# Features as 128k+p instead of 8p+k, and the work around it, in a two-layer diffusion backbone

## The chip, the cores and the metric

One Trainium2 chip, one core, one launch. The metric is the device time of the program in microseconds.

## What is computed

128 context tokens and 128 latent tokens of width 1024 go through two layers: HGRN2 (a gated linear recurrence, both directions), then neighbourhood attention, each followed by a mixture of experts; all in fp32. Cut to what the change touches:

```python
for l in range(2):
    sh1, sc1, g1, sh2, sc2, g2 = split(silu(c) @ ada_w[l] + ada_b[l], 6)     # one set for each token group
    x = x + g1 * mixer_l(rmsnorm(x, norm1_w[l]) * (1 + sc1) + sh1)
    h = rmsnorm(x, norm2_w[l]) * (1 + sc2) + sh2
    scores = sigmoid(h @ w_router)            # 64 experts, 8 groups, top 4 groups, top 6 experts
    hid = silu(h @ w_gate[e]) * (h @ w_up[e]) # 1024 -> 256 for each expert
    x = x + g2 * (sum_e((hid * combine[e]) @ w_down[e]) + shared_swiglu(h))
y = rmsnorm(x, final_norm_w)
```

## The kernel before

The activations stand transposed, features on partitions: `xT` and `hT` are [128, 8, 256], chunk k of partition p holds feature 8p+k, and the 256 columns are the two token groups. So weights are loaded as `(p k) n`, and where a product makes new features its stationary operand takes every eighth column: `late[:, h, k::K]` in `project_out`, `ws_dn[:, c, k::K]` in `shared_down`, `y[:, j, part, k::K]` in `combine`. An fp32 matmul is two records in the trace.

HGRN stage: blocks of `hgrn_w_in` and halves of the modulation weights `ada_w` (2 MB each) pass through a ring of five rooms. The table `ROUNDS` says which block, which items of the recurrence and how many modulation halves PE does in each round. `ada` is PE's part, `modulation` DVE's.

MoE (`experts_front`, `experts_pass`): `experts_front` turns `hT` into token rows, splits them into three bf16 parts (`h_tok`), routes and does the shared expert. Then 32 pairs of experts, 48 token slots each in half of the array, double buffered in `ring`. A pair on PE, in `down` and `gate_up`: gather of the next pair's tokens (48 bf16 matmuls of 96 columns), turn of `hid` (2 transposes of `hid[:, j, c::2]`), combine of the pair before (24 bf16 matmuls of 256 columns into PSUM banks 0 to 3), `turn_hots` (the one-hots times an identity, and times the 6 weight columns), down (8 fp32 matmuls of 512 columns), gate_up (32 of 256 columns). ACT does the silu and the high and middle parts of `y`, DVE the product `hid`, the rests of `y` and the next one-hots. SP loads gate and up of pair n+2 when `gate_up(n)` is done, and down when its product is done. After the last pair PE waits for the last part of `y` and does a combine, DVE adds the residual, ACT squares.

The end of the program: squares, `norm_sums` over all features broadcast to 128 partitions, root, reciprocal, products, gains, 16 transposes, four strided copies into `y_tok`, two DMAs from ACT's queue. Matmuls issued by the helper `mm` are L1288 in every view, ACT's copies L543; L1617 is the turn of `hid`, L885 the residual, L1170 `hid`, L840 the reciprocal, L554 the root, L393 SP's gate and up loads.

## Time and profile before

| | us |
|---|---|
| median of three runs | 1531.21 |
| lowest, highest | 1530.73, 1533.91 |
| profiled execution | 1534.29 |
| its span | 1532.5 |
| PE busy in it | 1485.4 |
| its mean granted clock of TensorE | 0.989 |

The profile comes from one execution, whose time stands 3.1 us above the median. Busy time overlaps where engines work beside each other. The two MoE stages take from about 273 to 815 us and from 972 to 1515 us of the span.

### The profile page before, as it was taken

To read this page: it belongs to the slowest core of one execution; us is meant where nothing else is said; L and a number is where in the kernel's file an instruction comes from. 1 tells how busy PE (TensorE), PEld (TensorE's weight loads), DVE (VectorE), ACT (ScalarE), POOL (GpSimd) and SP (SyncE) were. 2 spreads that over 40 slices of the span, in tenths; PEclk is the share of its full clock that TensorE was granted. 3 is DMA by queue.
4 is the path that set the end of the run, shared out by engine and by line. 5 is a ranking of instruction groups with operands and counts; after the bars stand their busy time and mean duration, and the time that the engine had idled before them with its cause. 6 is when DMAs were issued, how large, how long until landed. Compare 5 with 4: busy or idle time off the path is not lost.

```text
span 1532.5 us, 30939 instructions
## 1 busy us (share of the span) xinstructions
PE 1485.4 (97%) x13231; PEld 1056.8 (69%) x13231; DVE 461.1 (30%) x949; ACT 440.1 (29%) x1093; POOL 3.2 (0%) x17
## 2 busy tenths in 40 slices
PE   5999999999999999999998999999999999999996
PEld 3868779676666767666666859676767666676764
DVE  2244441622222222222223251612222222222224
ACT  2124331323232232322222131422222323222233
POOL 0000000000000000000000000000000000000000
PEclk8999999999999999999999999999999999999997
DMA  9976679489999999999999038469999999999970
GB/s 354 395 271 223 231 275 350 190 334 395 407 386 409 399 405 391 400 399 411 395 394 275 20 124 342 193 240 398 386 407 392 410 396 396 405 393 398 402 306 29
DMA packets 101443, 510.55 MB, mean 333 GB/s; under 512 B 11256, under 2 KB 19600, under 8 KB 52240
## 3 DMA queue, kind: packets, MB, share of 16 engines
q1 hardware_dynamic: 97440, 506.57, 83.7%
q10 hardware_dynamic: 3952, 3.24, 0.6%
q8 instruction: 39, 0.64, 0.2%
q14 instruction: 12, 0.10, 0.0%
HBM read 506.65 MB, written 3.15 MB: 333 GB/s over the span
## 4 chain that ended last, share of the span: by engine, by line
PE 94%; ACT 2%; DVE 2%; DMA 1%; SPq 1%; issue 0%; DVEq 0%; ACTq 0%
PE psum L1288 91%; PE psum L1617 1%; DMA arena<-in_ada_w 1%; ACT arena L543 1%; SPq L388 1%; DVE arena L840 0%; ACT arena L566 0%; PE psum L1499 0%; PE psum L1740 0%; PE psum L1784 0%; DVE arena L842 0%; DVE arena L1181 0%; DVE arena L1177 0%; ACT L554 0%; PE psum L1412 0%
## 5 line engine op out<-in xcount | busy, mean ns | idle before, releaser
L1288 PE MATMUL psum<-arena 128*64 128x256 f32 (+9 forms) x12948 | 1454.9, 335 | 25.5 <-DVE arena L1181 6.8
L1288 PEld LDWEIGHTS psum<-arena 128*64 128x64 f32 (+3 forms) x12948 | 1026.8, 135 | 447.6 <-issue 235.0
L543 ACT ACTIVATE arena<-psum 128x192 f32<-128x192 f32 (+5 forms) x550 | 198.3, 387 | 381.3 <-PE psum L1288 317.9
L1177 DVE TENSOR_TENSOR arena<-psum,arena 128x512 f32<-128x512 f32 x128 | 88.1, 688 | 315.8 <-ACT arena L543 315.8
L543 ACT ACTIVATE arena<-arena 128x512 bf16<-128x512 f32 (+1 forms) x144 | 87.5, 618 | 111.5 <-DVE arena L1177 108.9
L1181 DVE TENSOR_TENSOR arena<-arena 128x512 bf16<-128x512 f32 x128 | 88.7, 693 | 98.0 <-ACT arena L543 98.0
L705 ACT ACTIVATE arena<-psum 128x256 f32<-128x256 f32 x64 | 24.6, 385 | 299.1 <-PE psum L1288 299.1
L1170 DVE SCALAR_TENSOR_TENSOR arena<-arena,psum 128x256 f32<-128x256 f32 x64 | 30.8, 481 | 262.0 <-ACT arena L705 262.0
L1160 DVE COPY arena<-psum 128x192 f32<-128x192 f32 x128 | 39.8, 353 | 95.8 <-PE psum L1288 95.8
L885 DVE SCALAR_TENSOR_TENSOR arena<-psum,arena 128x128 f32<-128x128 f32 x64 | 18.0, 344 | 63.3 <-PE psum L1288 63.3
L550 ACT ACTIVATE arena<-arena 128x512 f32<-128x512 f32 x20 | 12.3, 629 | 73.2 <-DVE arena L885 72.2
L1617 PE MATMUL psum<-arena 128*128 128x128 f32 x128 | 29.9, 316 | 2.0 <-DVE arena L1170 2.0
L543 ACT ACTIVATION_READ_ACCUMULATOR arena<-psum 64x1 f32 x128 | 25.1, 196 | 0.8
L1072 DVE TENSOR_TENSOR arena<-arena 128x192 bf16<-128x192 f32 x64 | 22.5, 352 | 0.1
L1617 PEld LDWEIGHTS psum<-arena 128*128 128x128 f32 x128 | 20.2, 208 | 2.9 <-DVE arena L1170 2.9
L591 ACT ACTIVATE arena<-psum 128x1024 f32<-128x1024 f32 x8 | 8.2, 1025 | 45.0 <-PE psum L1288 45.0
L566 ACT ACTIVATE arena<-arena 128x128 f32<-128x128 f32 x32 | 12.8, 481 | 24.2 <-DVEq L877 16.4
L759 ACT ACTIVATE arena<-psum,arena 128x128 f32<-128x128 f32 x16 | 5.7, 366 | 33.9 <-DVE arena L1241 33.9
L840 DVE RECIPROCAL arena<-arena 128x256 f32<-128x256 f32 x5 | 8.8, 1754 | 19.1 <-ACT arena L554 11.3
L964 DVE TENSOR_TENSOR arena<-arena 128x1024 f32<-128x1024 f32 x12 | 14.1, 1219 | 0.1
L862 DVE STREAM_TRANSPOSE arena<-psum 128x256 f32<-128x256 f32 x12 | 5.3, 445 | 29.3 <-PE psum L1288 29.3
L842 DVE TENSOR_TENSOR arena<-arena 128x512 f32<-128x512 f32 (+1 forms) x15 | 12.2, 866 | 0.2
(142 smaller groups left out, 288.1 us busy)
## 6 DMA issues: line engine op xcount, KB each, us to landing
arena<-in_moe_w_gate SPq DMA_DIRECT2D x64, 2048.0 KB, 9.6
arena<-in_moe_w_up SPq DMA_DIRECT2D x64, 2048.0 KB, 14.1
arena<-in_moe_w_down SPq DMA_DIRECT2D x64, 2048.0 KB, 10.9
arena<-in_ada_w SPq DMA_DIRECT2D x24, 2048.0 KB, 12.6
arena<-in_hgrn_w_in SPq DMA_DIRECT2D x10, 2048.0 KB, 13.7
arena<-in_na_w_qkv SPq DMA_DIRECT2D x6, 2048.0 KB, 17.4
arena<-in_hgrn_w_out SPq DMA_DIRECT2D x1, 4096.0 KB, 13.6
arena<-in_na_w_o SPq DMA_DIRECT2D x1, 4096.0 KB, 13.9
```

What stands on the lines that cost most here:

```text
L388: sp.dma_start(room, stage_source(stages[n])).then_inc(stage_in[room_sem[n]], 16)
L543: return act.activation(out, in_, ACT.Copy, **kw)
L705: act.activation(silu[:, j], psum[:, 4, 0:F], ACT.Silu).then_inc(M.silu, 1)
L885: ins = dve.scalar_tensor_tensor(out=xT[:, k, at], in0=psum[:, k // 2, (k % 2) * NT + s * T:(k % 2) * NT + (s + 1) * T], scalar=g[:, k, s: ...
L964: ins = dve.tensor_tensor(dif[d].rearrange("p u (b t) -> p (u b) t", t=size), view, view[:, :, at:at + 1].broadcast_to(shape), ALU.subtract)
L1072: dve.tensor_tensor(hots, slots.unsqueeze(1).unsqueeze(1).broadcast_to(shape), ranks.unsqueeze(3).broadcast_to(shape), ALU.is_equal).then_ ...
L1160: ins = dve.tensor_copy(xg[:, j, 4:8, e * SPACE:e * SPACE + SLOTS], picked(1, e))
L1170: dve.scalar_tensor_tensor(out=hid[:, j], in0=silu[:, j], scalar=slot_w[:, j:j + 1], in1=psum[:, 4, F:2 * F], op0=ALU.mult, op1=ALU.mult). ...
L1177: dve.tensor_tensor(y_rest[:, at], psum[:, 6 + half, :], y[:, j, 0, at], ALU.subtract)\
L1181: ins = dve.tensor_tensor(y[:, j, 2, at], y_rest[:, at], y[:, j, 1, at], ALU.subtract)
L1288: return pe.matmul(out, lhsT, rhs, start=start, stop=stop, skip_group_check=True, **kw)
L1617: ins = pe.transpose(psum[:, 5, c * P:(c + 1) * P], hid[:, j, c::2], ident)
```

## The change

Feature 128k+p now stands on partition p in chunk k, so stationary operands are contiguous columns; expert weights keep `(p k)`, and the token rows are reordered as they leave PSUM (`piece`). Norm gains and modulation bias are loaded as rows and turned by PE. The one-hots are multiplied by an identity with the six weight columns beside it (`ident_w`, filled by `weight_columns`). Gate and up are one matmul of 512 columns. `hid` is written in two halves. In the last pair of an MoE `y` stays fp32, and `combine_last` takes eight fp32 matmuls. Two modulation halves move from the first two rounds to the place after the first MoE, and the rooms of the q, k, v blocks with them. The final norm works per token: rows weighted by the gain are turned, and the root of each token scales them as they leave PSUM.

```diff
+        WIDE = P + 6
+        ident_w = sc(2 * WIDE, (2, 2, WIDE), BF16)
...
+        y32 = y[:, 1, 0:2].rearrange("p i d -> p (i d)").bitcast(F32)
...
-        ROUNDS = [(0, [], [], 1), (1, [], [], 1), (2, [], [(0, DECAY)], 1), (3, [], [(0, 0)], 1), (4, [(0, 1)], [(0, 2)], 1),
+        ROUNDS = [(0, [], [], 0), (1, [], [], 0), (2, [], [(0, DECAY)], 1), (3, [], [(0, 0)], 1), (4, [(0, 1)], [(0, 2)], 1),
...
-        halves = [("ada", l, j, half) for l, j in parts[2:9] for half in range(2)]
+        halves = [("ada", l, j, half) for l, j in parts[2:8] for half in range(2)]
...
-            return src.rearrange("(p k) n -> p k n", p=P)
...
-        rooms = [(n - stages0 + 3) % 5 for n in range(stages0)] + [5, 6, 3, 4, 0, 1, 2, 3, 4, 0, 7, 8]
+            return src.rearrange("(k p) n -> p k n", p=P)
...
+        rooms = [(n - stages0 + 3) % 5 for n in range(stages0)] + [5, 6, 3, 4, 0, 1, 2, 3, 4, 0, 1, 2, 7, 8]
...
-            return n % 2, slice(4 * (n // 2), 4 * (n // 2) + 4)
+            return (n % 2, slice(64 * (n // 2), 64 * (n // 2 + 1)),
+                    psum[:, n, :].rearrange("p (q k) -> p k q", k=K))
...
-            (norm_w[:, 0:4:2, :], io["norm1_w"].rearrange("l (p k) -> p l k", p=P)),
...
+            (norm_rows[0:16], io["norm1_w"].rearrange("l (k p) -> (l k) p", p=P)),
...
+            (ada_rows, io["ada_b"].rearrange("l (j p) -> (l j) p", p=P)),
...
-            (router_w[:, 0], io["moe_w_router"][0].rearrange("(p k) e -> p k e", p=P)),
...
+            (router_w[:, 0], io["moe_w_router"][0].rearrange("(k p) e -> p k e", p=P)),
...
+            load_stage(qkv0 - 4)
+            load_stage(qkv0 - 3)
...
+            sp.wait_ge(moe[0].y_ps[1], more * PAIRS + (PAIRS - 1))
...
+            sp.wait_ge(*block_used(qkv0 - 4))
...
-            sp.wait_ge(moe[0].y_ps[1], more * PAIRS + (PAIRS - 1))
+            sp.wait_ge(*block_used(qkv0 - 3))
...
-            sp.wait_ge(*block_used(qkv0 - 2))
-            load_stage(qkv0 + 3)
-            sp.wait_ge(*block_used(qkv0 - 1))
-            load_stage(qkv0 + 4)
-            sp.wait_ge(*block_used(qkv0))
-            load_stage(qkv0 + 5)
-            sp.wait_ge(*block_used(qkv0 + 4))
+            for n in range(2, 5):
+                sp.wait_ge(*block_used(qkv0 + n - 4))
+                load_stage(qkv0 + n + 1)
+            sp.wait_ge(*block_used(qkv0 + 2))
...
-                    copy(h_tok[:, 0, a, ks], psum[:, n, :].rearrange("p (k t) -> p k t", t=P)).then_inc(M.htok, 1)
...
+                    copy(h_tok[:, 0, a, :, qs], turned).then_inc(M.htok, 1)
...
-                copy(onehot_t[:, j].rearrange("p a t -> p (a t)"), psum[:, 5, 0:NT])
+                turned = psum[:, 5, 0:2 * WIDE].rearrange("p (a n) -> p a n", a=2)
...
-                if not last:
-                    hots_turned(M, n + 1, 1 - j)
+                if last:
+                    copy(hot32, onehot_t[:, j].rearrange("p a t -> p (a t)"))
+                    act.wait_ge(M.y_ps[0], n + 1)
+                    copy(y32[:, 0:BLOCK], psum[:, 6, :]).then_inc(M.y_high, 2)
+                    act.sem_inc(M.y_mid, 2)
+                    return
+                hots_turned(M, n + 1, 1 - j)
...
-            squares(4)
-            norm_root(4)
-            norm(4, None)
-            for n in (0, 2):
-                act.wait_ge(yt_ps, n + 1)
-                copy(y_tok[:, n // 2, :, 0:4].rearrange("s p k -> s k p"),
-                     psum[:, n, :].rearrange("s (k p) -> s k p", p=P)).then_inc(yt_sb, 1)
-            act.wait_ge(yt_sb, 4)
-            for a, name in enumerate(("out_prompt", "out_sample")):
-                act.dma_start(io[name][0], y_tok[:, a].rearrange("s p k -> s (p k)")).then_inc(y_out, 16)
+            def weighted(i):
+                for k in (2 * i, 2 * i + 1):
+                    copy(hT[:, k], xT[:, k], scale=norm_w[:, 4, k:k + 1]).then_inc(h_done[0], 1)
...
+            act.activation(lb_t[:, 0:1], eps, ACT.Sqrt)
+            for i in range(4):
+                act.wait_ge(resid, 12 + i + 1)
+                if i < 2:
+                    weighted(i)
+                act.activation(sq[:, 2 * i:2 * i + 2], xT[:, 2 * i:2 * i + 2], ACT.Square).then_inc(sq_done, 1)
+            weighted(2)
+            act.wait_ge(ssum, 5)
+            act.activation(tok_rstd, psum[:, 0, 0:4:2], ACT.Sqrt, scale=1.0 / D, bias=eps).then_inc(root, 1)
+            act.wait_ge(yt_ps, 2)
+            act.wait_ge(x_normed, 13)
+            for n in range(2):
+                copy(y_tok[:, 0, n * BLOCK:(n + 1) * BLOCK], psum[:, 4 + n, :], scale=tok_rstd[:, 0:1]).then_inc(act_c, 1)
+            act.wait_ge(act_c, 4)
+            act.dma_start(io["out_prompt"][0], y_tok[:, 0]).then_inc(y_out, 16)
...
+            dve.tensor_copy(ada_b.rearrange("p l j k -> p (l j k)"), psum[:, 5, 0:96])
...
+            def weight_columns(expert, j):
...
+                dve.tensor_copy(ident_w[:, j, :, P:WIDE].rearrange("p a (e i) -> p a e i", e=2), weights)
...
-                modulation(9 + 2 * m)
+                modulation(8 + 3 * m)
+                dve.tensor_copy(ident_w[:, :, :, 0:P].rearrange("p j a n -> p (j a) n"),
+                                ident.unsqueeze(1).broadcast_to((P, 4, P)))
...
-                    dve.tensor_tensor(h_rest[:, a, ks], psum[:, n, :].rearrange("p (k t) -> p k t", t=P),
-                                      h_tok[:, 0, a, ks], ALU.subtract).then_inc(M.h_rest, 1)
+                    dve.tensor_tensor(h_rest[:, a, :, qs], turned, h_tok[:, 0, a, :, qs], ALU.subtract).then_inc(M.h_rest, 1)
...
+                    weight_columns(next_expert, 1 - j)
...
-                dve.scalar_tensor_tensor(out=hid[:, j], in0=silu[:, j], scalar=slot_w[:, j:j + 1],
-                                         in1=psum[:, 4, F:2 * F], op0=ALU.mult, op1=ALU.mult).then_inc(M.hid, 1)
-                if next_expert is not None:
-                    gathered(M, n + 1, 1 - j)
+                dve.scalar_tensor_tensor(out=hid[:, j].rearrange("s (c p) -> s p c", c=2),
+                                         in0=silu[:, j].rearrange("s (p c) -> s p c", c=2), scalar=slot_w[:, j:j + 1],
+                                         in1=psum[:, 4, F:2 * F].rearrange("s (p c) -> s p c", c=2),
+                                         op0=ALU.mult, op1=ALU.mult).then_inc(M.hid, 1)
+                if next_expert is None:
+                    dve.sem_inc(M.y_rest, 2)
+                    dve.wait_ge(M.y_ps[1], n + 1)
+                    dve.tensor_copy(y32[:, BLOCK:D], psum[:, 7, :]).then_inc(M.y_low, 1)
+                    return
+                gathered(M, n + 1, 1 - j)
...
-            normed(4)
-            norm(4, None)
-            for n in (1, 3):
-                dve.wait_ge(yt_ps, n + 1)
-                dve.tensor_copy(y_tok[:, n // 2, :, 4:8].rearrange("s p k -> s k p"),
-                                psum[:, n, :].rearrange("s (k p) -> s k p", p=P)).then_inc(yt_sb, 1)
+            dve.wait_ge(resid, 16)
+            for k in (6, 7):
+                dve.tensor_scalar(hT[:, k], xT[:, k], norm_w[:, 4, k:k + 1], None, ALU.mult).then_inc(h_done[1], 1)
+            dve.wait_ge(root, 5)
+            dve.reciprocal(tok_rstd, tok_rstd).then_inc(x_normed, 1)
+            dve.wait_ge(yt_ps, 2)
+            dve.wait_ge(x_normed, 13)
+            for n in range(2):
+                dve.tensor_scalar(y_tok[:, 1, n * BLOCK:(n + 1) * BLOCK], psum[:, 6 + n, :], tok_rstd[:, 1:2], None,
+                                  ALU.mult).then_inc(yt_sb, 1)
...
-                        ins = mm(psum[32 * c:32 * c + 32, ada_bank(part), 0:2 * P], cond_act[:, half * (K // 2) + i, :],
-                                 w[:, i, 2 * P * c:2 * P * (c + 1)], half == 0 and i == 0, half == 1 and i == K // 2 - 1)
+                        ins = mm(psum[32 * c:32 * c + 32, ada_bank(part), 0:2 * P].rearrange("p (k q) -> p k q", k=K),
+                                 cond_act[:, half * (K // 2) + i, :],
+                                 w[:, i].rearrange("p (k q) -> p k q", k=K)[:, :, 32 * c:32 * c + 32], half == 0 and i == 0, half == 1 and i == K // 2 - 1)
...
-                            ins = mm(psum[:, k // 2, (k % 2) * NT:(k % 2 + 1) * NT], late[:, h, k::K], src[:, h],
+                            ins = mm(psum[:, k // 2, (k % 2) * NT:(k % 2 + 1) * NT], late[:, h, k * P:(k + 1) * P], src[:, h],
...
-                    mm(psum[:, 5, a * P:(a + 1) * P], onehot[:, j, a], ident_b, True, True)
-                for a in range(2):
...
-                    ins = mm(psum[:, 5, NT:NT + 6], onehot[:, j, a], weights.rearrange("p e i -> p (e i)"),
-                             a == 0, a == 1)
+                    ins = mm(psum[:, 5, a * WIDE:(a + 1) * WIDE], onehot[:, j, a], ident_w[:, j, a], True, True)
...
-                        ins = mm(psum[:, k // 2, (k % 2) * NT:(k % 2 + 1) * NT], y[:, j, part, k::K],
-                                 onehot_t[:, j].rearrange("p a t -> p (a t)"), False, False)
...
+                        mm(psum[:, k // 2, (k % 2) * NT:(k % 2 + 1) * NT], y[:, j, part, k * P:(k + 1) * P],
+                           onehot_t[:, j].rearrange("p a t -> p (a t)"), False, False)
...
+            def combine_last(M, n):
...
+                pe.wait_ge(M.y_high, n * 2 + 2)
+                pe.wait_ge(M.y_low, n + 1)
+                for k in range(K):
+                    ins = mm(psum[:, k // 2, (k % 2) * NT:(k % 2 + 1) * NT], y32[:, k * P:(k + 1) * P], hot32, False, False)
+                    if k % 2:
...
-                            ins = mm(psum[at, 4, w * F:(w + 1) * F], xg[:, j, k, at],
-                                     ring[:, j, 2 * e + w, k * F:(k + 1) * F], k == 0 and w == 0, k == K - 1)
...
+                        ins = mm(psum[at, 4, :].rearrange("p (w f) -> p w f", w=2), xg[:, j, k, at],
+                                 ring[:, j, 2 * e:2 * e + 2, k * F:(k + 1) * F], k == 0, k == K - 1)
...
-                    ins = pe.transpose(psum[:, 5, c * P:(c + 1) * P], hid[:, j, c::2], ident)
+                    ins = pe.transpose(psum[:, 5, c * P:(c + 1) * P], hid[:, j, c * P:(c + 1) * P], ident)
...
-            norm_sums(4)
-            for n in range(4):
-                for i in range(4):
-                    k = 4 * (n % 2) + i
-                    h_chunk(4, k)
-                    ins = pe.transpose(psum[:, n, i * P:(i + 1) * P], hT[:, k, (n // 2) * T:(n // 2 + 1) * T], ident)
-                ins.then_inc(yt_ps, 1)
...
+            def token_sums(i):
+                pe.wait_ge(sq_done, 16 + i + 1)
+                for k in (2 * i, 2 * i + 1):
+                    for a in range(2):
+                        ins = mm(psum[:, 0, 2 * a:2 * a + 2], sq[:, k, a * T:(a + 1) * T], ones[:, 0:2],
+                                 k == 0 and a == 0, k == K - 1)
+                if i == 3:
+                    ins.then_inc(ssum, 1)
...
+            def token_rows(i):
+                for k in (2 * i, 2 * i + 1):
+                    if k < 6:
+                        pe.wait_ge(h_done[0], 16 + k + 1)
+                    else:
+                        pe.wait_ge(h_done[1], 16 + k - 5)
+                    for a in range(2):
+                        ins = pe.transpose(psum[:, 4 + 2 * a + k // 4, (k % 4) * P:(k % 4 + 1) * P],
+                                           hT[:, k, a * T:(a + 1) * T], ident)
+                if i in (1, 2):
+                    ins.then_inc(yt_ps, 1)
...
+            for i in range(2):
+                token_rows(i)
+                token_sums(i)
+            token_sums(2)
+            token_rows(3)
+            token_sums(3)
+            token_rows(2)
```

PE's order at the start of the HGRN stage, after the first modulation halves (32x256 is half a modulation part by 16, 128x256 by 32 one block). Before:

```order
L1288 MATMUL psum<-arena 32x256 x64
L1288 MATMUL psum<-arena 128x256 x32
L1446 MATMUL psum<-arena 128x8 x3
L1288 MATMUL psum<-arena 32x256 x16
L1288 MATMUL psum<-arena 128x256 x32
L1288 MATMUL psum<-arena 32x256 x16
L1288 MATMUL psum<-arena 128x256 x32
```

Now:

```order
L1333 MATMUL psum<-arena 32x256 x64
L1333 MATMUL psum<-arena 128x256 x32
L1495 MATMUL psum<-arena 128x8 x3
L1333 MATMUL psum<-arena 128x256 x64
L1333 MATMUL psum<-arena 32x256 x16
```

The two halves between the first three blocks are gone. PE's order in one pair of the loop (128x96 is the gather, 128x256 the combine, 64x512 down, 64x256 gate_up). Before:

```order
L1617 MATMUL psum<-arena 128x128 x2
L1288 MATMUL psum<-arena 128x256 x24
L1288 MATMUL psum<-arena 128x128 x2
L1288 ISA
L1288 MATMUL psum<-arena 128x6
L1288 ISA
L1288 MATMUL psum<-arena 128x6
L1625 ISA
L1288 MATMUL psum<-arena 64x512 x8
L1596 ISA
L1288 MATMUL psum<-arena 64x256 x32
```

Now:

```order
L1667 MATMUL psum<-arena 128x128 x2
L1333 MATMUL psum<-arena 128x256 x24
L1333 MATMUL psum<-arena 128x134 x2
L1675 ISA
L1333 MATMUL psum<-arena 64x512 x8
L1647 ISA
L1333 MATMUL psum<-arena 64x512 x16
```

Four matmuls of the one-hots became two, 32 of gate_up 16.

PE's order at the end of the program, from the last pair's down product on (128x128 are transposes). Before:

```order
L1288 MATMUL psum<-arena 64x512 x8
L1666 REGISTER_ALU
L1666 COMPARE_AND_BRANCH
L1665 UNCONDITIONAL_BRANCH
L1668 ISA
L1288 MATMUL psum<-arena 128x256 x32
L1784 MATMUL psum<-arena 128x128 x16
```

Now:

```order
L1333 MATMUL psum<-arena 64x512 x8
L1637 ISA
L1333 MATMUL psum<-arena 128x256 x8
L1717 REGISTER_ALU
L1717 COMPARE_AND_BRANCH
L1716 UNCONDITIONAL_BRANCH
L1848 MATMUL psum<-arena 128x128 x4
L1333 MATMUL psum<-arena 128x2 x4
L1848 MATMUL psum<-arena 128x128 x4
L1333 MATMUL psum<-arena 128x2 x8
```

The last combine (24 of the 32) became 8 matmuls, and the transposes stand between the sums of the norm.

## Rows read from the trace of the kernel before

**Rows 1.** the page: busy time by engine, and the chain that ended last
```profile
PE 1485.4 (97%) x13231; PEld 1056.8 (69%) x13231; DVE 461.1 (30%) x949; ACT 440.1 (29%) x1093; POOL 3.2 (0%) x17
...
PE 94%; ACT 2%; DVE 2%; DMA 1%; SPq 1%; issue 0%; DVEq 0%; ACTq 0%
```

**Rows 2.** timeline of SP's queue, one pair apart: start us, us, line, tiles
```profile
499.40 0.37 SPq L393 DMA_DIRECT2D arena<-in_moe_w_gate  x1
...
515.14 0.37 SPq L393 DMA_DIRECT2D arena<-in_moe_w_gate  x1
```

**Rows 3.** DMA issues from 500 to 516 us: KB each, median us to landing
```profile
arena<-in_moe_w_up SPq DMA_DIRECT2D x2, 2048.0 KB, 14.1
```

**Rows 4.** stretches: PE, PEld, DVE, ACT, POOL busy; clock, DMA share, GB/s
```profile
502.00:503.00 1.00, 1.00 (x11) 1.00 (x10) 0.02 (x1) 0.09 (x1) 0.00 (x0) 1.00 0.88 287
...
507.00:508.00 1.00, 1.00 (x8) 0.41 (x6) 0.69 (x1) 0.28 (x1) 0.00 (x0) 1.00 1.01 426
```

**Rows 5.** PE by shape, 320 to 776 us (29 pairs): busy us, mean
```profile
L1288 PE MATMUL psum<-arena 128*64 128x256 f32 x1852 | 205.3, 378 | 0.0
...
L1288 PE MATMUL psum<-arena 128*128 128x256 bf16 x696 | 81.3, 272 | 0.0
...
L1617 PE MATMUL psum<-arena 128*128 128x128 f32 x58 | 13.5, 315 | 0.0
...
L1288 PE MATMUL psum<-arena 128*128 x58 | 5.5, 166 | 0.0
```

**Rows 6.** weight loads by shape, whole run: `hid` (strided), attention (contiguous)
```profile
L1617 PEld LDWEIGHTS psum<-arena 128*128 128x128 f32 x128 | 20.2, 208 | 2.9 <-DVE arena L1170 2.9
...
L1740 PEld LDWEIGHTS psum<-arena 128*128 128x128 f32 x32 | 3.5, 140 | 2.3 <-issue 2.3
```

**Rows 7.** timeline in one pair: the turn of `hid`, then the combine
```profile
501.20 0.47 PE L1617 MATMUL psum<-arena 128*128 128x128 f32 x2
...
501.51 3.52 PE L1288 MATMUL psum<-arena 128*128 128x256 bf16 x30
```

**Rows 8.** stretches of PE: 256 fp32 columns, strided (first) and contiguous weights
```profile
236.00:260.00 24.00, 24.00 (x102) 1.00 1.03 416
...
825.00:849.00 24.00, 24.00 (x113) 1.00 0.81 267
```

**Rows 9.** start: two stretches, then PE's first projection in the timeline
```profile
14.00:18.00 4.00, 3.13 (x42) 1.00 1.11 318
...
18.00:22.00 4.00, 1.77 (x32) 1.00 1.04 412
...
34.46 13.81 PE L1288 MATMUL psum<-arena 128*128 128x256 f32 x49 [3.50 <-ACT arena L566]
```

**Rows 10.** the modulation matmuls, 24 half parts, by shape
```profile
L1288 PE MATMUL psum<-arena 128*32 128x256 f32 x768 | 47.4, 390 | 7.4 <-DMA arena<-in_ada_w 6.8 <-DVE arena L862 0.7
```

**Rows 11.** end of the first MoE, timeline: [idle before <-releaser]
```profile
809.72 12.60 PE L1288 MATMUL psum<-arena 128*128 128x256 bf16 x104 [3.58 <-DVE arena L1181]
...
818.76 0.47 ACT L554 ACTIVATE arena<-psum,arena 128x256 f32<-128x256 f32 x1 [0.57 <-PE psum L1288]
```

**Rows 12.** end of the program, the same view
```profile
1509.02 9.22 PE L1288 MATMUL psum<-arena 128*128 128x256 bf16 x40 [3.23 <-DVE arena L1181]
1510.56 1.13 DVE L885 SCALAR_TENSOR_TENSOR arena<-psum,arena 128x128 f32<-128x128 f32 x4 [1.59 <-PE psum L1288]
...
1514.40 1.13 DVE L885 SCALAR_TENSOR_TENSOR arena<-psum,arena 128x128 f32<-128x128 f32 x4 [0.15 <-PE psum L1288]
...
1525.26 1.09 DVE L1281 COPY arena<-psum 128x512 f32<-128x512 f32 x1 [0.57 <-PE psum L1784]
...
1528.45 0.45 ACTq L818 DMA_DIRECT2D out_sample<-arena  x1
```

**Rows 13.** durations used as prices: a PSUM copy, the product `hid`
```profile
8.26 0.69 DVE L895 COPY arena<-psum 128x512 f32<-128x512 f32 x1 [3.08 <-PE psum L1295]
...
499.67 0.48 DVE L1170 SCALAR_TENSOR_TENSOR arena<-arena,psum 128x256 f32<-128x256 f32 x1 [3.94 <-ACT arena L705]
```

106 lines of the change are left out of this document (58 added, 48 removed).

## The prediction

> **What bounds the kernel now.** I read the page first: PE is busy 97% of the span and carries 94% of the chain that ended last [rows 1]. So a microsecond counts only if it leaves PE's own sequence of matmuls or one of PE's few waits. Then the loop over the expert pairs: SP issues the gate load of successive pairs 15.74 us apart [rows 2], 64 pairs make 1007 of the 1532.5 us, and PE is busy throughout the stretches shown [rows 4]. The rival for the bound is the DMA. It is busy all the time in the loop, at 426 GB/s while gate and up are multiplied and at 287 GB/s in the combine [rows 4], but the load of `up` lands 14.1 us after its issue [rows 3], and PE wants it two pairs less one gate_up later, some 2 x 15.7 - 7 = 24 us. About 10 us of slack stand between the queue and PE. Last the waits at the ends: 3.58 and 3.23 us before the last combine of each MoE [rows 11, 12], and a long serial tail after it.
>
> **Weight loads with a stride.** The output projection reads `late[:, h, k::K]`, an fp32 column every 32 bytes. From 236 to 260 us, 102 records less the 2 that reach in from outside give 24/100 = 0.240 us for each record; the same shape with contiguous weights gives 24/111 = 0.216 us [rows 8]. PE issues two records per fp32 matmul, so one projection of 64 matmuls loses 128 x 0.024 = 3.0 us, two of them 6.0. The shared down projection has the same stride and 32 records twice: 1.5 us. All of this is PE's own time before the waits that follow, so it should be gained whole: **-7.4 us**, bounds -6 and -8.
>
> **The pair loop, 62 full turns.** (a) The turn of `hid` reads every second column. Its loads take 208 ns, contiguous ones 140 [rows 6]; two transposes take 0.31 us until the combine starts [rows 7], and 0.22 would be two at 0.109, half of a 256-column record [rows 8]. That is 0.08 us a pair, bounds 0.02 and 0.14 (twice 68 ns). (b) The combine's 24 matmuls take 81.3/29/24 = 0.117 us each with tails [rows 5], against 0.108 for 256 columns; most of the difference is tail, so I take 0.02 us, bounds 0 and 0.2. (c) Two 6-column matmuls go and 12 columns are added; they show 5.5/29 = 0.19 us a pair, nearly all latency [rows 5]: 0.05 us, bounds 0 and 0.12. (d) Gate and up become one product of 512 columns. The columns are as many, only the fixed cost of 16 matmuls goes: 205.3/29 = 7.08 us a pair for 64 records with tails [rows 5] against 32 x 0.432 = 6.9. I take 0.05, bounds -0.05 and 0.1. Sum 0.20, rounded down to 0.19 a pair: **-11.8 us**, range -6 to -19. DVE gets a 12-element copy before the one-hots, where it has microseconds to spare, and writes `hid` in two interleaved halves. A copy with such scattered writes took 1.09 us for 512 elements against 0.69 [rows 12, 13], so `hid` may grow from 0.48 to 0.68 us. It is finished at 500.15, the turn starts at 501.20 [rows 7, 13]; hidden, except in the last pair of each MoE, where no gather covers it: +0.4 us in all.
>
> The Trainium skill has a rule against (a): "SBUF — State Buffer", section "Door 1: The DMA port swizzle", says SBUF has 16-byte lines and that a stride is free as long as two accesses share a line, which holds for every second fp32. By it (a) gives nothing and the sum is 5 us smaller. The row says 208 ns against 140, so the trace disagrees and I go by the row.
>
> **Modulation moved.** One half of a modulation part takes PE 47.4/24 = 1.97 us with tail [rows 10], 1.87 net. Two halves leave the first two rounds of the HGRN stage, where PE has no wait: **-3.7 us**. They return after the first MoE. There PE's last down product ends at 809.72 - 3.58 = 806.14 [rows 11]. Now ACT and DVE each copy one half of the result in fp32; a copy is 0.69 us [rows 13], so the combine starts near 806.9, not 809.7. Eight fp32 matmuls take 8 x 0.43 = 3.5 us, to 810.4; the two halves end at 814.1; the eight norm sums, which were done as the squares arrived, take 3.5 us, to 817.6. Their squares are ready before that, as the residual starts 3.2 us sooner: 2.8 from the combine's start, and 0.4 because it now follows that start by about 1.1 us (two fp32 matmuls of 0.43 and a drain), where it took 1.54 with six bf16 ones [rows 12]. So the root comes at 817.8 instead of 818.76 [rows 11]: **-1.0 us**, bounds 0 and -3. SP's loads of the q, k, v blocks move too: the first now follows the last but one down product instead of the gate_up ahead of it, the second and third wait for PE's two moved halves, near 812 and 814. PE wants the first after the norm, near 822, and each further one 14 us later (64 records of 0.216); a load takes 14.1 us at worst from a full queue [rows 3], and this queue is empty. So they are hidden, with some 8 us to spare.
>
> **The end.** The residual starts the same 3.2 us sooner (it is at 1510.56 now) [rows 12]; its last step ends at 1514.40 + 1.13 = 1515.53 and then near 1512.3. From there to the last output's issue the kernel takes 12.9 us now: root of 256 columns, reciprocal, products, gains, 16 transposes, copies of 1.09 us with strided writes [rows 12]. Afterwards the weighted rows are turned beside the squares, the sums are per token (2 columns), root and reciprocal have 2 elements. What is left: a square 0.8, sums 0.9 to 2.2 (two clocks), root, reciprocal and their hand-overs 0.7, two copies of 0.69 with hand-over 1.5, issue: 4.3 to 5.6 us. Each output now has its own queue, which ends the run some 0.3 us nearer to the issue. 12.9 - 4.9 + 0.3 = 8.3, with 3.2: **-11.5 us**, bounds -10 and -13.
>
> **Start.** Norm gains and modulation bias were 32-byte pieces and are now rows of 512 bytes. Between 14 and 18 us the DMA moves 318 GB/s, just behind it 412 [rows 9]: 4 x 94/412 = 0.9 us lost, and 0.2 for the pieces elsewhere. PE's first projection, at 34.46 after 3.50 us of idleness, is put down to ACT's gains [rows 9], but those were written from 32 us on, and the block of `hgrn_w_in`, fifth in the queue behind those pieces, landed at 34.4: it came last, so **-1.1 us**. The bound the other way: the router's weights turn from 2 KB into 256-byte pieces, up to 2.6 us of queue, but behind the block that PE waits for; and PE now waits for the small vectors before its first norm sums, with some 10 us of waiting behind it. Range +0.5 to -2.5.
>
> **Routing fronts.** ACT copies and DVE subtracts four PSUM tiles, now read with stride, and DVE fills the wide identity. At the price of scattered writes this were +0.4 us for each of eight steps and up to 1.7 us on PE per front; a strided PSUM read alone I expect to cost little. I take **+0.3 us** per front, bounds 0 and 1.7.
>
> **Sum.** -7.4 - 11.8 + 0.4 - 3.7 - 1.0 - 11.5 - 1.1 + 0.6 = -35.5 us. The profiled execution took 1534.29 us, 3.1 above the median of the runs shown, 1531.21; the terms are differences, so I take them off the median: **1495.7 us**.
>
> **Rivals.**
> - *The DMA becomes the bound of the loop.* If the queue cannot deliver a pair in under 15.7 us, the shorter turns of PE only eat the 10 us of slack. At 0.19 us a pair 31 pairs use 6 us of it, so even then PE should not wait; only a gain twice as large would. If it bites from the first pair: 1495.7 + 11.8 = 1507.5. The Trainium skill, "DMA: Bandwidth & Descriptors", section "Where 436 GB/s comes from", gives 435 GB/s as ceiling; by it 6.29 MB take an estimated 14.5 us, below PE's turn. The trace's 426 GB/s agrees.
> - *The stride is not what slows the loads.* Then -7.4 and the 5 us of (a) fall away: 1508.1. Against it stand two stretches of one shape at one clock [rows 8].
> - *The product `hid` takes over the loop, slower than before.* DVE's scattered write is on the path gate_up, ACT, DVE, turn. It has 1.05 us of cover; to undo 35.5 us over 62 pairs it must take 0.48 + 1.05 + 0.57 = 2.1 us. At 3 us the run would be 1495.7 + 62 x 1.47 = 1587. The dearest scattered write in the rows costs 0.8 ns an element more, a tenth of that.
> - *It does more.* If PE's clock holds through the end and the combine gains its 0.2 us, 12 us more: 1484.
>
> **How the numbers follow.** Forecast 0.82 (its own range 1488 to 1503), DMA 0.06, stride 0.06, more 0.03, `hid` 0.02, an unseen standstill 0.01. The range 1487 to 1505 takes in the forecast and the nearer part of its neighbours. This kernel's measurement can tell 0.2%, 3 us; faster 0.97, same 0.01, slower 0.02.
>
> **What would show it.** Records 0.216 us apart in both output projections; 15.55 us between SP's gate issues; no PE idle before L1333 in the loop on DMA or DVE; the wait before the last combine near 0.8 us; root of the next norm about 1 us after the sums; some 8 us from the last residual to the end. I am wrong if PE waits for a load in the loop, if the turn of `hid` still takes 0.31 us, or if the first projection starts later than 34.

## The result and the profile after

The changed kernel takes 1506.5 us (median of 4 runs, 1505.4 to 1507.4), the kernel before 1531.8 in the same series: ratio 0.9833, 95% interval 0.9816 to 0.985, or 25.3 us less. The forecast was 35.5 us less, 1495.7, with 1505 as the upper end of its range. So the sign was right, but 10.2 us of the forecast gain did not come, and the time lies above the range. (It misses the forecast by 10.8 us; the other 0.6 is the median of the kernel before, 1531.8 here and 1531.2 in the runs that the forecast started from.) The profiled execution took 1505.39 us with a span of 1503.6; against [rows 1]'s execution (span 1532.5) that is 28.9 us less.

The page of the changed kernel, busy time and chain, the answer to [rows 1]:

```profile
PE 1464.5 (97%) x11057; PEld 861.0 (57%) x11057; DVE 468.9 (31%) x1002; ACT 436.9 (29%) x1088; POOL 3.2 (0%) x17
...
PE 93%; SPq 2%; ACT 2%; DVE 1%; DMA 1%; issue 0%; DVEq 0%; ACTq 0%
...
L1203 DVE SCALAR_TENSOR_TENSOR arena<-arena,psum 128x256 f32<-128x256 f32 x64 | 43.2, 675 | 254.3 <-ACT arena L713 254.3
```

PE is still the bound. The last row, from the page's list of groups, is the product `hid`, now with its scattered write: 0.675 us each, against 0.48 [rows 13].

The pair loop, PE by shape from 320 to 776 us (busy us, mean ns), the answer to [rows 5]:

```profile
L1333 PE MATMUL psum<-arena 128*64 128x512 f32 x1402 | 307.7, 593 | 0.0
L1333 PE MATMUL psum<-arena 128*128 128x256 bf16 x713 | 82.9, 272 | 0.0
L1667 PE MATMUL psum<-arena 128*128 128x128 f32 x58 | 11.6, 281 | 0.0
L1333 PE MATMUL psum<-arena 128*128 128x134 bf16 x60 | 8.4, 221 | 0.0
```

The column of idle time shows 0.0, as before: no wait in the loop. SP's queue, two gate issues one pair apart, the answer to [rows 2]:

```profile
504.16 0.37 SPq L401 DMA_DIRECT2D arena<-in_moe_w_gate  x1
...
519.75 0.37 SPq L401 DMA_DIRECT2D arena<-in_moe_w_gate  x1
```

They stand 15.59 us apart, 0.15 less than the 15.74 of [rows 2]; the forecast was 0.19. From the starts of the records in the trace, medians over 29 pairs: turn of `hid` 0.303 to 0.236 us, combine 2.640 to 2.628, one-hots 0.235 to 0.210, gate_up 7.020 to 6.973, gather and down unchanged.

Three stretches (PE busy and records, PEld, DVE, ACT, POOL, clock, DMA share, GB/s): the second output projection, gate_up, and the combine, the answers to [rows 8] and [rows 4]:

```profile
925.00:949.00 24.00, 24.00 (x113) 20.95 (x112) 3.38 (x12) 1.51 (x3) 0.00 (x0) 1.00 0.97 378
...
502.00:503.00 1.00, 1.00 (x8) 0.33 (x6) 0.00 (x0) 0.00 (x0) 0.00 (x0) 1.00 0.99 418
507.00:508.00 1.00, 1.00 (x12) 0.89 (x10) 0.00 (x0) 0.00 (x0) 0.00 (x0) 1.00 0.93 344
```

The output projection now has the 113 records in 24 us that only contiguous weights had before. PE is busy in all of each stretch, and the loop showed no wait for a load: the DMA did not become the bound.

Now the place where the gain went. PE at the end of MoE 0, timeline of the changed kernel: start, us, then idle before and its releaser, the answer to [rows 11]:

```profile
785.89 0.44 PE L1667 MATMUL psum<-arena 128*128 128x128 f32 x2 [1.18 <-DVE arena L1203]
...
793.43 3.69 PE L1333 MATMUL psum<-arena 128*128 128x256 f32 x16 [0.88 <-DVE arena L1210]
799.31 12.71 PE L1333 MATMUL psum<-arena 128*32 128x256 f32 x144 [2.19 <-issue]
812.51 0.67 PE L1333 MATMUL psum<-arena 128*128 128x256 f32 x2 [0.49 <-ACT arena L573]
```

The last combine starts 0.88 us after the down product, as forecast (3.58 before). But behind it PE stands still for 2.19 us, and the row names no engine and no DMA, only "issue". PE's own sequencer explains it. Line 1716 is the branch past the code of the extra passes, which these inputs don't need; the row has minimum, median and maximum in ns, then the starts of first and last:

```profile
L1716 PEldq COMPARE_BRANCH  x2: 3540/4161/4782, 794.4 to 1488.4; - x2
```

It begins at 794.36, while PE still works off the last combine (until 797.12), and takes 4.78 us, to 799.14; PE's next matmul starts at 799.31. Its twin in the kernel before:

```profile
L1665 PEldq COMPARE_BRANCH  x2: 3342/4778/6213, 803.4 to 1502.8; - x2
```

There it ran from 803.35 to 809.57, beside the last down product and the long wait for DVE, and the combine of [rows 11] starts at 809.72. DVE's last step ended at 808.62 + 0.69 = 809.31 in that trace. So the row's "<-DVE L1181" hid a second releaser that came 0.26 us later. The Trainium skill says of this, "Runtime: NRT & Kernel Launch", section "Instruction fetch mechanics", that a taken branch whose target lies outside the code already fetched makes the engine wait for a fetch by DMA. This case's traces agree. Not taken, this branch took 71 or 77 ns (below); taken it took 3.3 to 6.2 us. And the jump back in the loop over the pairs, which is also a taken branch, took 0.21 us and came with no packet of code at all: the DMA list of the loop, 337.5 to 767 us, has one queue only, while the stretch of the branch has a packet of code of 16 KB (queue 8). The loop's branch (350 to 775 us), the queues in the loop, and queue 8 from 794.36 to 799.14 (packets, MB, share):

```profile
L1701 PEldq COMPARE_BRANCH  x13: 207/208/213, 374.9 to 749.2; - x13
...
q1 hardware_dynamic: 22465, 173.19, 98.9%
...
q8 instruction: 1, 0.02, 1.5%
```

By these rows a taken branch is not dear as such, but one to code that has to be fetched is.

The stretch behind that standstill, same columns as above:

```profile
799.30:808.30 9.00, 8.99 (x82) 6.24 (x83) 0.62 (x2) 1.44 (x2) 0.00 (x0) 0.81 0.62 207
```

The granted clock is 0.81 there, and two modulation halves and eight norm sums took 9.0 us where 7.2 were forecast. PE had been idle for 2.19 us just before. The second trace of this same kernel (the last experiment) shows how far executions differ here: there the branch took 4.34 us, PE waited 1.75, and the clock behind it stayed at 1.00.

```profile
798.71 11.07 PE L1333 MATMUL psum<-arena 128*32 128x256 f32 x144 [1.75 <-issue]
...
799.00:808.00 9.00, 9.00 (x116) 6.17 (x112) 1.98 (x3) 2.05 (x3) 0.00 (x0) 1.00 0.72 245
```

In the traces of the changed kernel and its variants the 9 us behind the wait for this branch had a clock of 0.81 eight times, after waits of 2.19 to 3.67 us, and 1.00 after waits of 1.75 and 1.37 and where the branch is gone. The kernel before has 0.77 behind its 3.58 us.

The end of the program, PE's timeline, against [rows 12]:

```profile
1487.66 3.69 PE L1333 MATMUL psum<-arena 128*128 128x256 f32 x16 [0.89 <-DVE arena L1210]
1492.02 0.66 PE L1848 MATMUL psum<-arena 128*128 128x128 f32 x4 [0.67 <-ACT arena L550]
...
1493.80 1.85 PE L1333 MATMUL psum<-arena 128*128 128x2 f32 x16
...
1496.79 0.98 PE L1848 MATMUL psum<-arena 128*128 128x128 f32 x4
...
1499.24 0.37 SPq L516 DMA_DIRECT2D out_sample<-arena  x1
```

Again a gap, 0.67 us, until the branch is through (1488.42 + 3.54 = 1491.96), though the row names ACT, whose first pieces were ready by 1490.9. Behind it PE works without a pause until the last rows are turned.

The start: PE's first projection, and two stretches, against [rows 9]:

```profile
34.23 14.18 PE L1333 MATMUL psum<-arena 128*128 128x256 f32 x64 [2.21 <-DMA arena<-in_hgrn_w_in]
...
14.00:18.00 4.00, 4.00 (x22) 3.04 (x24) 0.00 (x0) 0.19 (x1) 0.00 (x0) 1.00 1.03 418
30.00:34.00 4.00, 2.01 (x20) 0.65 (x12) 1.69 (x7) 0.95 (x3) 0.00 (x0) 0.67 1.18 299
```

The DMA moves 418 GB/s where it moved 318, as forecast, but the projection starts only 0.23 us sooner, and later than the 34 that the prediction had named as a sign of being wrong.

### The profile page after: what moved, and what is told of

The parts are those of the page before. It is cut to its first block, busy times and chain, and to the rows that moved or that the text cites. A ratio compares the mean times of both kernels' runs of the same rounds, so it can differ in the third digit from the quotient of the medians.

```text
span 1503.6 us, 26618 instructions
## 1 busy us (share of the span) xinstructions
PE 1464.5 (97%) x11057; PEld 861.0 (57%) x11057; DVE 468.9 (31%) x1002; ACT 436.9 (29%) x1088; POOL 3.2 (0%) x17
## 4 chain that ended last, share of the span: by engine, by line
PE 93%; SPq 2%; ACT 2%; DVE 1%; DMA 1%; issue 0%; DVEq 0%; ACTq 0%
PE psum L1333 91%; SPq L439 1%; PE psum L1667 1%; DMA arena<-in_hgrn_w_in 1%; SPq L396 1%; ACT arena L550 0%; DVE arena L862 0%; PE psum L1548 0%; PE psum L1792 0%; DVE arena L907 0%; ACT arena L573 0%; ACT L561 0%; PE psum L1848 0%; DVE arena L864 0%; PE psum L1461 0%
## 5 line engine op out<-in xcount | busy, mean ns | idle before, releaser
L1333 PE MATMUL psum<-arena 128*128 128x96 bf16 (+9 forms) x10772 | 1440.2, 368 | 18.5 <-DMA arena<-in_ada_w 5.3
L1333 PEld LDWEIGHTS psum<-arena 128*128 128x128 bf16 (+4 forms) x10772 | 835.9, 124 | 615.0 <-issue 522.9
L550 ACT ACTIVATE arena<-psum 128x192 f32<-128x192 f32 (+6 forms) x546 | 195.6, 385 | 371.1 <-PE psum L1333 312.8
L1203 DVE SCALAR_TENSOR_TENSOR arena<-arena,psum 128x256 f32<-128x256 f32 x64 | 43.2, 675 | 254.3 <-ACT arena L713 254.3
L550 ACT ACTIVATE arena<-arena 128x512 bf16<-128x512 f32 (+2 forms) x140 | 86.3, 625 | 107.9 <-DVE arena L1216 105.5
L1667 PE MATMUL psum<-arena 128*128 128x128 f32 x128 | 25.6, 282 | 2.4 <-DVE arena L1203 2.4
L550 ACT ACTIVATION_READ_ACCUMULATOR arena<-psum 64x1 f32 x128 | 25.3, 197 | 0.8
L1667 PEld LDWEIGHTS psum<-arena 128*128 128x128 f32 x128 | 13.1, 142 | 4.1 <-DVE arena L1203 4.1
L989 DVE TENSOR_TENSOR arena<-arena 128x1024 f32<-128x1024 f32 x12 | 14.1, 1219 | 0.1
L957 DVE TENSOR_SCALAR arena<-arena 128x256 f32<-128x256 f32 x16 | 5.5, 409 | 19.1 <-ACT arena L598 19.1
## 6 DMA issues: line engine op xcount, KB each, us to landing
arena<-in_moe_w_up SPq DMA_DIRECT2D x64, 2048.0 KB, 14.1
```

The costliest lines, as they stand in the source:

```text
L550: return act.activation(out, in_, ACT.Copy, **kw)
L1203: dve.scalar_tensor_tensor(out=hid[:, j].rearrange("s (c p) -> s p c", c=2), in0=silu[:, j].rearrange("s (p c) -> s p c", c=2), scalar=slo ...
L1333: return pe.matmul(out, lhsT, rhs, start=start, stop=stop, skip_group_check=True, **kw)
L1667: ins = pe.transpose(psum[:, 5, c * P:(c + 1) * P], hid[:, j, c * P:(c + 1) * P], ident)
```

## The experiments

Times are medians, and each ratio is against the kernel before in the same series; each kernel is compared with the changed one (1506.5, ratio 0.9833, and 1507.0, again 0.9833, in a second series).

**The branch ahead of the last combine.** The sequence of matmuls is the same.

```
                 n0, load0 = r * PAIRS, r * (PAIRS // 2) + 1
+                if not isinstance(r, int):
+                    combine_last(M, n0 - 1)
...
                 down(M, n0 + PAIRS - 1, 1, load0 + PAIRS // 2 - 1, None)
-                combine_last(M, n0 + PAIRS - 1)
...
                 with pe.If(more > 0):
                     with pe.Fori(0, more) as r:
                         experts_pass(M, r + 1)
-                return more
+                combine_last(M, more * PAIRS + PAIRS - 1)
```

> The changed kernel, but PE reads the number of extra passes and branches past their code before the last combine instead of behind it. Theory 'branch': in the changed kernel this branch takes 4.8 us after MoE 0 and 3.5 us after MoE 1, of which 2.19 and 0.67 us stand as PE waits behind the last combine. Put ahead, it runs beside the last down product and DVE's copy: the last combine of MoE 0 starts some 2 us after the down product instead of 0.88, the wait of 2.19 us before the modulation half is gone, and so is the one of 0.67 us at the end. Sum -1.0 - 0.7 = -1.7 us, -3.3 if the clock holds behind it: 1503 to 1505 us. Rival 'late weights' (the half waits for its own load, issued late by SP): the wait stays where it is and the time is 1506.5. Rival 'clock alone': the wait goes but the halves and sums still take 9.06 us.

1505.4 us (0.9828, 0.9815 to 0.9842). PE at the end of MoE 0, and the branch:

```profile
796.38 16.40 PE L1333 MATMUL psum<-arena 128*128 128x256 f32 x160 [3.67 <-issue]
...
L1717 PEldq COMPARE_BRANCH  x2: 3500/4833/6166, 789.9 to 1484.6; - x2
```

The wait moved with the branch, so it is the branch's; the weights of the half were not late. But it took 6.17 us now, not 4.8, and PE waited 3.67: after MoE 0 nothing is won (27.2 us from the turn of the last pair to the next projection, against 26.6). This is the kernel before once more, wait (3.58) and branch (6.21) alike. After MoE 1 the 0.67 us are gone.

**No branch on PE.**

```
                 pe.wait_ge(M.table, 1)
-                more = pe.value_load(extra[0:1, 0:1].bitcast(I32), min_val=0, max_val=PASSES - 1)
-                with pe.If(more > 0):
-                    with pe.Fori(0, more) as r:
-                        experts_pass(M, r + 1)
-                return more
```

> The changed kernel without the extra passes on PE: neither the read of their number nor the branch past them (with these inputs there is none, so the products are the same; the general case is left out). Theory 'branch': no PE wait before the modulation half after MoE 0 (now 2.19) nor before the token rows at the end (now 0.67): -2.9 us, -4.5 if the clock then stays up: 1502 to 1503.6 us. Rival 'late weights': the wait of 2.19 us stays, 1506.5.

1500.7 us (0.9796, 0.9783 to 0.981): 5.8 less than the changed kernel, more than expected. PE after MoE 0:

```profile
794.38 14.69 PE L1333 MATMUL psum<-arena 128*128 128x256 f32 x160 [0.89 <-DVE arena L1210]
809.55 14.82 PE L1333 MATMUL psum<-arena 128*128 128x256 f32 x65 [0.48 <-ACT arena L573]
```

Combine, halves, sums and halves follow each other without a gap, and at the full clock. From the turn of the last pair (786.85) to the next projection 22.70 us pass, against 26.62 in the changed kernel and 24.52 in its second trace, where the clock stayed up: the branch costs 1.8 to 3.9 us there, and 1.0 at the end.

**Loads held back around the branch.** SP issues two modulation halves and the first q, k, v block only when the last combine has ended.

> The changed kernel with SP's loads of two modulation halves and the first q, k, v block held back until the last combine of MoE 0 has ended, so that little runs on the DMA while PE branches. If the branch's code has to pass the same DMA as the weights, it takes the 3.5 us of MoE 1 instead of 4.8, and PE's wait falls from 2.19 to about 0.9 us. If its length has to do with the place in the code, it stays at 4.8. Later PE waits for the late loads: some 10 to 15 us are lost there and say nothing.

```profile
800.31 7.40 PE L1332 MATMUL psum<-arena 128*32 128x256 f32 x80 [1.37 <-issue]
...
L1715 PEldq COMPARE_BRANCH  x2: 3460/3711/3962, 796.2 to 1495.9; - x2
```

The branch took 3.96 us and PE's wait fell to 1.37. In ten traces with weights in flight it took 4.3 to 6.2 us after MoE 0, and 3.3 to 3.8 wherever it was taken in or behind MoE 1, where no load is in flight. The packets in the traces say where the difference lies. In each of these 27 taken branches there is a packet of 16 KB of code. From the branch's start to the last such packet's start 0.93 to 1.45 us pass without loads, 1.61 in this run, and 1.83 to 3.73 beside the loads; the packet takes 0.88 to 1.32 us, and from its end to the branch's end it is 1.35 to 1.53 us, with or without loads. So the branch waits for its code, and what varies is how late that packet starts; that it is the weights' packets that hold it back fits all 27, but is argued. (This version took 1514.6 us in its one execution: PE then waited 3.2 and 2.2 us for the late loads.)

**The usual case in line.** Can the branch be left out and the extra passes kept? PE's code is laid out so that the usual case falls through:

```
+                if then is not None:
+                    with pe.If(more < 1):
+                        combine_last(M, PAIRS - 1)
+                        then()
...
                 with pe.If(more > 0):
                     with pe.Fori(0, more) as r:
                         experts_pass(M, r + 1)
...
+                    if then is not None:
+                        combine_last(M, more * PAIRS + PAIRS - 1)
+                        then()
+                if then is None:
+                    combine_last(M, more * PAIRS + PAIRS - 1)
```

After MoE 0 `then` is the whole rest of PE's program, which so stands there twice; after MoE 1 it is None.

> The changed kernel with PE's code laid out so that the usual case falls through after MoE 0: where no extra pass is wanted PE goes straight on to the last combine and the rest of the program, and the extra passes stand behind that, with a second copy of the rest; after MoE 1 the branch stands ahead of the last combine. Theory 'branch' (the last runs: without it 1500.7 us; a branch ahead of the combine is hidden after MoE 1, where it takes 3.5 us, and not after MoE 0, where it takes 6.2): from the turn of the last pair to the next projection 22.7 us as in the kernel without a branch, against 26.6, and 22.5 from the turn of the last pair to the end, against 23.5: 1501 us. Rival 'code': any conditional code costs PE a fetch there, also one that isn't jumped over, or the much longer program costs elsewhere: 1503 to 1507 us.

1502.2 us (0.9797, 0.9785 to 0.981), by its ratio the same as without any branch (0.9796). The branch after MoE 0, which is now not taken:

```profile
L1719 PEldq COMPARE_BRANCH  x1: 71/71/71, 790.6 to 790.6; - x1
```

From the turn of the last pair to the next projection it is 22.70 us again: a conditional body costs PE no wait there as long as it isn't jumped over. After MoE 1 the branch stands ahead of the combine (3.72 us, hidden but for 0.15). The second copy is jumped over in 3.31 us, from 1491.63 on, beside PE's last products and before the outputs are issued at 1495.12. In this trace, and in that of the version with all together, the prompt's output lands 5.6 us after its issue, where it is 3.8 without a branch and 3.1 in the version with one half first; why is open. The paths of the extra passes stand in the program, but these inputs never take them.

**The two modulation halves back in the HGRN stage**, with rooms, loads and counts as before the change.

> The changed kernel with the two modulation halves back in the first two HGRN rounds, with rooms and loads as before the change. By the prediction's working the move is worth 3.7 us there and costs 2.3 after MoE 0 (root of norm 2 some 3.3 us sooner instead of 1.0), so undoing it should cost 1.4: 1507.9. Theory 'branch and clock': behind MoE 0 the halves take 5.3 us at the lower clock, not 3.7, and fill no wait, since PE's branch makes its wait whatever follows; undoing gives +3.8 in the HGRN stage and -5.4 behind MoE 0: -1.6, 1504.9 us.

1512.2 us (0.9866, 0.9851 to 0.9882; single executions from 1509.5 to 1514.5, the profiled one the slowest), 5.7 more than the changed kernel: both expectations fell, 1507.9 by the prediction's working and 1504.9 by what the result had shown. PE at the start and after MoE 0:

```profile
54.63 5.92 PE L1328 MATMUL psum<-arena 128*128 128x256 f32 x13 [3.17 <-DMA arena<-in_hgrn_w_in]
...
811.26 9.08 PE L1328 MATMUL psum<-arena 128*128 128x256 f32 x80 [3.12 <-ACT arena L553]
```

With one more 2 MB load ahead of it the second HGRN block lands late and PE waits 3.17 us, where the changed kernel waits 0.30 us and the one before not at all; behind that wait its projection took 16.97 us, at a clock of 0.82, for 13.9. And the wait for the branch is 3.12 us, with no halves behind it. So the move is worth more than my 1.4 us, for a reason that I had not seen: it also keeps the start's queue short. The kernel before has the same order of loads and no wait; there the half lands at 46.01 us and the block at 51.75, here at 49.21 and 54.59. By the router's run below it is the change itself that lengthens the queue: the router's weights are now loaded in 256-byte pieces.

**All strided weight reads back**, `late[:, h, k::K]`, `ws_dn[:, c, k::K]`, `y[:, j, part, k::K]` and `hid[:, j, c::2]`.

> The changed kernel with the four strided weight reads of before the change (output projections, shared down product, turn of hid, combine), and nothing else undone, so the features come out in another order than the reference's: this is a measurement of the reads alone. Theory 'stride' (from the two traces: 3.1 us in the second output projection, 0.86 in a shared down product, 0.067 + 0.012 us in a pair): 2 x 3.1 + 2 x 0.86 + 62 x 0.079 = +12.8 us, 1519.3. Rival 'lines': only the reads 32 bytes apart cost (7.9 us), the turn of hid at 8 bytes is free and its gain came from elsewhere: 1514.4.

The features come out in another order here, which changes the routing of the second layer, and an extra pass of 0.5 ms ran there. So the total (2025 us) says nothing, and the stages must. PE by shape in the loop, a stretch of the first output projection, and the branch:

```profile
L1667 PE MATMUL psum<-arena 128*128 128x128 f32 x58 | 13.5, 315 | 0.0
...
236.00:260.00 24.00, 24.00 (x102) 23.89 (x101) 3.38 (x12) 1.89 (x3) 0.00 (x0) 1.00 1.03 404
...
L1716 PEldq COMPARE_BRANCH  x2: 77/3144/6212, 801.3 to 1503.1; - x2
```

Both are the rows of before [rows 5, 8] to the last record: 102 records, 13.5 us. The output projections take 34.79 and 34.89 us, as before, against 31.7 at full clock and 31.79; the turn 0.303, the combine 2.640, a pair 15.67 us. The stride costs what it seemed to cost, that of 8 bytes too. By accident the run also has a branch that isn't taken, after MoE 1: 77 ns.

**Gate and up as two products of 256 columns.**

```
-                        ins = mm(psum[at, 4, :].rearrange("p (w f) -> p w f", w=2), xg[:, j, k, at],
+                            ins = mm(psum[at, 4, w * F:(w + 1) * F], xg[:, j, k, at],
```

> The changed kernel with gate and up as two products of 256 columns again, 32 instead of 16 instructions a pair. By the traces the one product gave 0.047 us a pair: +2.9 us, 1509.4, and 7.02 instead of 6.97 us from the first gate_up record to the turn or gather. Rival: those 0.047 come from elsewhere in the pair (the data's arrival): 1506.5.

1507.8 us (0.9841, 0.9827 to 0.9855), and 1509.6 (0.9847, 0.9831 to 0.9863) in a second series, whose trace is used:

```profile
L1333 PE MATMUL psum<-arena 128*64 128x256 f32 x1856 | 205.5, 378 | 0.0
...
503.85 0.37 SPq L401 DMA_DIRECT2D arena<-in_moe_w_gate  x1
...
519.50 0.37 SPq L401 DMA_DIRECT2D arena<-in_moe_w_gate  x1
```

15.65 us a pair (15.644 by the median) and 7.02 us of gate_up, as expected: 16 instructions fewer are worth 0.047 us, 3 ns each. By the times the two kernels can't be told apart (the intervals overlap); it is the trace that shows it.

**The start: three runs on why the first block still lands at 34.2 us.** The router's loads in the middle of the HGRN stage:

> The changed kernel with the two router weights and biases (now 256-byte pieces) loaded in the middle of the HGRN stage instead of behind the first hgrn_w_in block. Theory 'small pieces': their packets run beside the end of the block that PE waits for, which is why the first projection starts only 0.23 us sooner than before the change where 1.1 was forecast; without them it starts near 33.3 instead of 34.23, the wait of 0.30 us after it is gone: -1.3 us, 1505.2. Rival 'queue': the block is bound by the 2 KB packets ahead of it and lands at 34.2 all the same: 1506.5.

1506.9 us (0.984, 0.9826 to 0.9853); the first projection starts at 34.23. The router's pieces are not the cause of that. But the second block lands at 44.50 us, not at 48.94: those pieces cost some 4.4 us of queue, behind the block, where the prediction had said up to 2.6. The changed kernel pays 0.30 us for it, the one with the halves moved back 3.17. Everything behind the block held back until it has landed:

> The changed kernel, but SP issues the loads behind the first hgrn_w_in block (lower bounds, router, tables, states) only when that block has landed. Theory 'shared queue': in the traces of both kernels 12.20 MB have moved by 34.2 us, in the changed one 0.4 MB more by 30 us, and the packets behind the block run while its last ones are under way; that is where the gain of the 512-byte rows went. With them held back the block lands 0.9 us sooner and the first projection starts near 33.3 us. Later loads land 1 to 2 us later, and PE may wait for the second block near 49 us, so the whole may stay as it is. Rival 'order': the block's landing doesn't depend on what is behind it, the first projection starts at 34.2 again.

1509.0 us (0.9848, 0.9832 to 0.9865); the block lands at 34.42, though the DMA is busy for only 0.59 of the stretch from 30 to 34 us. So the packets behind don't hold it up. The one small vector that both kernels load in 4-byte pieces, as a row:

```
-            (gn_w, io["hgrn_gn_w"].rearrange("a d -> d a")),
+            (norm_rows[40:41], io["hgrn_gn_w"]),
...
+            dve.tensor_copy(gn_w, psum[:, 5, 136:137])
```

> The changed kernel with the last small vector, hgrn_gn_w, loaded as one row of 512 bytes and turned on PE with the others, instead of as 128 pieces of 4 bytes, which both kernels load (with one packet for each by the trace, most of them between 8 and 12 us, where the DMA moves 379 GB/s instead of 410 and more). Theory 'small pieces on few engines': those 128 pieces hold back the DMA engines that carry them, and the big blocks land with their slowest engine; the first hgrn_w_in block then lands 0.5 to 1.5 us sooner than at 34.2 and the first projection starts at 33 to 33.7; PE's wait before the turn of the vectors (2.2 us) is shorter. Rival: the landing stays at 34.2, and this vector isn't what sets it.

1504.9 us (0.982, 0.9807 to 0.9834), and PE at the start:

```profile
10.45 0.42 PE L1344 MATMUL psum<-arena 96*128 96x96 f32 x1 [0.73 <-DMA arena<-in_hgrn_gn_w]
...
33.81 15.88 PE L1334 MATMUL psum<-arena 128*128 128x256 f32 x64 [2.22 <-DMA arena<-in_hgrn_w_in]
```

The wait for the vectors shrinks from 2.25 to 0.73 us. The block lands at 33.76 us, 0.42 sooner, just short of the half microsecond that I had set as the least. But in the nine other traces with the start of the changed kernel it landed between 33.92 and 35.03, so one trace doesn't tell 0.42 us from chance (in the version below with this vector as a row it was 33.89), nor do the times: 1504.9 against 1507.0 in the same series, with intervals that overlap. That the vector is a part of the cause is not shown, and the rest stays open. In every trace used here but one, one of the first blocks lands 6.0 to 6.7 us behind the one before it instead of 5.1, and it is the block in flight when PE's first fetch of 16 KB of code comes (one packet, 1.03 us), or the one that starts right on it; where the fetch came earliest, at 20.70 us, the block before was the long one. That this fetch delays it is argued, not shown.

**One half ahead of the last combine**, in a free PSUM bank, on top of the code in line:

```
                     with pe.If(more < 1):
+                        ada(18)
                         combine_last(M, PAIRS - 1)
...
             def rest():
-                ada(18)
                 ada(19)
```

> The version with PE's code in line (1502.2 us), and the first modulation half after MoE 0 multiplied ahead of the last combine, into the PSUM bank of the turned rows that is free there, so that it fills PE's wait of 0.88 us for the copies of the last pair. Theory 'PE is the bound there': everything behind is PE's own work up to the root, so 0.88 us are gained: 1501.4. Rival 'residual': the combine starts 1.0 us later, and residual, squares and norm sums follow it; then the gain is nothing, 1502.2, with a new wait before the norm sums.

1501.4 us (0.9797, 0.9784 to 0.9811). By the ratio this is the version in line (0.9797) once more. The trace shows the gain: the 0.88 us of waiting are filled, and from the turn of the last pair to the next projection it is 21.92 us for 22.70.

**All together**: code in line, that half first, and the last vector as a row.

> The version with PE's code in line and one half ahead of the last combine (1501.4 us), with hgrn_gn_w as a row too. By the theory of the small pieces 0.5 to 1.5 us less, 1500.4; by its rival 1501.4.

1500.8 us (1500.4 to 1501.2), ratio 0.9787, 0.9774 to 0.98, in a series in which the changed kernel took 1507.0. PE from the turn of the last pair of MoE 0:

```profile
785.40 0.44 PE L1668 MATMUL psum<-arena 128*128 128x128 f32 x2 [1.18 <-DVE arena L1204]
785.68 21.16 PE L1334 MATMUL psum<-arena 128*128 128x256 bf16 x200
807.33 16.98 PE L1334 MATMUL psum<-arena 128*128 128x256 f32 x75 [0.48 <-ACT arena L573]
```

The 26.6 us (24.5 in its second trace) of the changed kernel are 21.9 now. This version beats both kernels; the extra passes stand in its program, though no run here takes them.

**The changed kernel once more.**

> The changed kernel itself a second time, on one chip with the versions. Theory 'clock': its stages repeat within 0.1 us except for two, the first projection (14.1 us in the profile shown, 17.0 us in others of kernels with the same start) and the first output projection (33.3 us shown, 31.7 in others), which depend on the granted clock of that execution; the sum is 1506.5 within 1 us, and PE's wait behind the last combine of MoE 0 is 2.2 to 3.6 us. Rival: the two stages repeat exactly as in the profile shown and the differences are the kernels' own.

1507.0 us (0.9833, 0.9819 to 0.9846). The pair takes 15.60 us in both traces. The first projection took 15.9 us instead of 14.1, the first output projection 31.68 instead of 33.32, the branch after MoE 0 4.34 us instead of 4.78, and PE's wait behind the last combine 1.75 us instead of 2.19, just below what I had expected. Over the traces of the changed kernel and its variants the first projection took 14.1 to 16.9 us, and 17.0 in the kernel before.

## Why the prediction was wrong, step by step

- **The bound, and the DMA as its rival**: right. No wait in the loop, loads as early as before (`up` lands 14.1 us after its issue in both), and 403 GB/s on average from 337.5 to 767 us.
- **Strided loads, -7.4** (its parts add up to 7.5): right. 3.1 us in the second output projection (3.0), 0.86 us in each shared down product (0.75). The first output projection gave 1.5 us in the profiled execution only, because its first records ran at a clock of 0.66; in nine traces of its variants and in its own second one it takes 31.7 us, 3.1 less than before, and in two others 32.7 and 33.3.
- **The stride rule against (a)**: the row was the better guide. Loads 8 bytes apart take 208 ns, contiguous ones now 142, and undoing the change brings the 0.303 us back.
- **The pair loop, -11.8**: right in kind, 0.15 us a pair instead of 0.19, so -9.3, inside its bounds. (a) 0.067 for 0.08, (b) 0.012 for 0.02, (c) 0.025 for 0.05, (d) 0.047 for 0.05. Each of the four prices was a little too high, which came to 2.5 us over 62 pairs.
- **`hid`**: 0.675 us as forecast, hidden; the last pair waits 0.18 us longer in each MoE.
- **Modulation, -3.7 and -1.0**: the failed step. The combine does start 0.88 us behind the down product, as the step "so the combine starts near 806.9, not 809.7" has it. But "to 810.4; the two halves end at 814.1" puts nothing between the combine and the halves, and takes the full clock for all that follows. It read the wait of [rows 11] as DVE's alone. The branch ended at 809.57 in the same wait, and I never looked at what PE's sequencer does between the last down product and the combine. By moving the combine ahead of that branch, the change took away its cover: 2.19 us in the open, and 9.0 us at the clock of 0.81 for 7.2. From the turn of the last pair to the next projection it was 26.6 us instead of 23.5, 3.2 more where 1.0 less was forecast; in the second trace, with 1.75 us of waiting and the full clock, 24.5. The kernel before had run this stretch at 0.77, so a part of the clock's loss is not new; the forecast had taken it as gone. By the stages the branches cost 1.8 to 3.9 us there and 1.0 at the end; by the medians 5.8. To an unseen standstill the prediction had given 0.01. The two halves did leave the HGRN stage for 3.7 us.
- **The end, -11.5**: it was -10.0 from the turn of the last pair. The residual came sooner, by 2.8 us at its start and 3.6 at its last step (3.2 forecast), but from its last step to the last output's issue took 6.2 us, not 4.9. I had counted root, copies and hand-overs and let PE's part run beside them; 16 transposes and 32 records of two columns, 0.10 us each, are 5.7 us of PE's own there, and the branch's 0.67 stand ahead of them. No row had shown the 0.9 to 2.2 us that the prediction took for the sums. From the last residual to the end it is 10.6 us, where the prediction had named some 8 as its sign. The 0.3 us for separate queues did not come (4.05 us from the last issue to the end before, 4.35 now).
- **Start, -1.1**: it was -0.2. The rate of the DMA rose as said, the landing didn't follow: a rate over all its engines is not the landing of one block.
- **Fronts, +0.6**: it was 0 (20.24 us from the front's first matmul to the first gather, before and after); reading PSUM with a stride costs nothing that shows here.
- **Off the median**: the two profiled executions differ by 28.9 us, the medians by 25.3, and 2.9 of it is the clock of the first projection, 17.0 us in one and 14.1 in the other.

The branches 3 to 6 (2.8 to 4.9 by the stages of the two traces, 5.8 by the medians), the loop 2.5, the end without the branch 0.8, the start 0.9, the fp32 combine 0.2 (3.69 us for 3.5), less 0.6 for the fronts: some 7 to 10 of the 10.2 us. The rest is open.

## What to carry to other kernels

When a wait is to be shortened, look for everything that ends in it, not only for the releaser that the row names: engines' sequencers, their register loads and branches above all. Here one row said "issue" and the others named DVE or ACT, and in all of them the branch ended last. A jump past a large body should stand where the engine has to wait anyway, or not be in the usual path at all: give the rare case the jump. The jump back of a loop is another matter, at 0.21 us.

## What the hardware showed that I had not expected

A taken branch past the code of four unrolled pairs took PE 3.3 to 6.2 us, the jump back in the loop of two pairs 0.21, one not taken 0.071 or 0.077. Nearly all the spread of the long ones lies in how late their packet of code starts. PE's sequencer runs only some 3 us ahead of its matmuls (the branch began at 794.36 while the combine ran until 797.12), so neither of the two positions tried hid it all after MoE 0. And the stride that slows PE's weight reads doesn't slow the DMA: the single microseconds shown have 344 GB/s in the combine now and 287 before [rows 4], but over all the pairs between 318 and 776 us, from start, length and size of every packet, the combine has 351 GB/s now, 349 before and 354 in the run with the strides back, beside 420 in gate_up in all three.
